# Routing ops of a mixture-of-experts kernel trimmed and interleaved, and one expert's weight loads moved behind a gather

## The chip, the cores and the metric

The kernel runs on one core of a Trainium2 chip. The metric is the device time of one execution in microseconds (us), the median over the runs. TensorE (PE) does matmuls and transposes, VectorE (DVE) and ScalarE (ACT) elementwise work, GpSimd (POOL) issues the indirect transfers, and SyncE (SP) issues most of the others. Engines meet only at semaphores.

## The reference, cut to what matters

One layer of a diffusion model over 640 tokens of width 1024 (512 latent, 128 context). After attention, convolution and a LayerNorm, every token passes through a hierarchical mixture of experts: the best of 4 groups, then the two best of the group's 4 experts.

```
g_prob = softmax(t @ wg + bg);  g_p, g_idx = top_k(g_prob, 1)
e_prob = softmax(take_along_axis(e_logits, g_idx)); e_p, e_idx = top_k(e_prob, 2)
ids = g_idx * 4 + e_idx
hid = einsum("nd,edf->nef", t, w_exp_in); a, up = split(hid, 2)
out = einsum("nef,efd->nd", silu(a) * up * gate, w_exp_out)
```

The kernel does not compute all 16 experts for all tokens. It makes for each expert a list of up to 128 tokens, gathers their rows, and works on these alone.

## The kernel before

Everything is written out by hand: the order of the instructions on each engine is that of the code, and waits are on counted semaphores. Matrices are split into a high and a low part (`w_hi` on ACT, `w_lo` on DVE), and three products stand for one.

The 640 tokens are five tiles of 128, n = 0 to 4 (NT = 5). In the stage before the experts, PE computes the output projection `mix_out(n)`, DVE makes the LayerNorm of tile n out of it and then `h2`, the rows that the experts read. PE turns these (`turn_h2`), ACT copies them (`h2_copy`), PE multiplies by the router's weights (`router`, `router_fold`), and DVE chooses:

- `choose(n)` on DVE (L1477): a chain of 13 small ops in which each waits for the one before (`link`), from the logits to the one-hot of both choices, `both` and `before`, which release `rank(n)` on PE (L2210).
- `put(n)` on DVE (L1505): the token's place in its experts' lists out of `rank(n)`'s sums, `slot_hot` (for the list, `fill(n)` on PE, L2217) and `hot_0` (L1516, L1517), a one-hot of the tokens that go to expert 0. `put(2)` stands between the halves of tile 4's LayerNorm.
- `gather_first(n)` on PE (L2195): expert 0's rows are not fetched; they are summed out of the tiles in SBUF by matmuls with `hot_0`.
- The list for the experts 1 to 15 (`list_s`, L1634 and L1635) is ready after `fill(4)`.

In the experts' stage POOL fetches the rows of expert c by an indirect DMA (`gather`, L743) from the DRAM copy of h2, which POOL stored tile by tile (L735). The gather of expert 1 waits for the stores of all tiles, for the list, and for ACT's last `normed`. When it has landed (`s_hg[1]`), PE turns the rows (`turn_rows(1)`, L2277), ACT and DVE split them (`gathered_hi`, `gathered_lo`, L1074 and L1608), and so on, with `down(c - 1)` at the end of each round. Before that, PE has the sums of expert 0 (`up_first(0, 0, 0)` and `up_first(0, 0, 1)`, L2290 to L2302), whose low parts DVE makes in four pieces, the last behind a wait for the issue of gather 1 (`s_gi`, L1649).

SP issues in one queue, in the order of the code: `expert_in(e, h)` half h (1 MB) of expert e's input weights, into one of 7 half homes (L567); `expert_out(e)` (1 MB, L593); `x1_away(j)` (1 MB, L607), which puts away rows whose space the halves of experts 4 and 5 take. `expert_in(5, 0)` waits until both have landed.

Of the kernel before, what the change touches and what calls it, by code (L numbers as in the profile page):

```python
# [5 lines left out]
def build(nc, ins, outs):  # L6
# [6 lines left out]
    ALU = mybir.AluOpType  # L13
# [8 lines left out]
    P = 128  # L22
# [28 lines left out]
    NR = 24  # L51
# [21 lines left out]
    with ctx:  # L73
# [114 lines left out]
        e_num = cols[:, 10:10 + 2 * NT].rearrange("p (t c) -> p t c", t=NT)  # L188
        e_at = cols[:, 20:28].bitcast(mybir.dt.uint32)
        g_num = cols[:, 28:29]  # L190
        over_hot = raw[:, 1, 0:2 * NT * P].rearrange("p (i s) -> p i s", i=2 * NT)
# [276 lines left out]
        def _(sp):  # L468
# [757 lines left out]
        def _(dve):  # L1226
# [249 lines left out]

            def choose(n):  # L1477

                lg = logits[:, n, :]
# [3 lines left out]
                link(V.tensor_tensor(lg, PS[:, 2 if n == NT - 1 else 6, 0:NR], rb[:, :], ALU.add))  # L1483
                link(V.max(g_top[:, n, :], lg[:, 0:E_AT]))
                link(V.max_index(g_at, g_top[:, n, :], lg[:, 0:E_AT]))
# [3 lines left out]
                link(V.max(e_top[:, n, :], e_open))  # L1489
                link(V.max_index(e_at, e_top[:, n, :], e_open))  # L1490
                link(V.tensor_copy(e_num[:, n, :], e_at[:, 0:2]))
                link(V.tensor_tensor(OH[:, n], const[:, C_NUM:C_NUM + NE].unsqueeze(1).to_broadcast([P, 2, NE]),
                                     e_num[:, n, :].unsqueeze(2).to_broadcast([P, 2, NE]), ALU.is_equal))
                if n == 0:
                    link(V.memset(before[:, 0, :], 0.0))
                else:
                    dve.wait_ge(s_pos, n)
                link(V.tensor_tensor(both[:, n % 2, :], OH[:, n, 0, :], OH[:, n, 1, :], ALU.add))
# [6 lines left out]
            def put(n):  # L1505

                dve.wait_ge(s_pos, n + 1)
                src = PS[:, 3 if n == NT - 1 else 6, 32:32 + NE]
                link(V.tensor_tensor(at_pos, OH[:, n], src.unsqueeze(1).to_broadcast([P, 2, NE]), ALU.mult))
                link(V.tensor_reduce(place[:, n, :], at_pos, AX.X, ALU.add))  # L1510
# [4 lines left out]
                dve.wait_ge(s_plr, n + 1)  # L1515
                link(V.tensor_scalar(hot_0[:, n, :], slot_hot[:, n % 2, 0, :], OH[:, n, 0, 0:1], None, ALU.mult))  # L1516
                V.scalar_tensor_tensor(out=hot_0[:, n, :], in0=slot_hot[:, n % 2, 1, :], scalar=OH[:, n, 1, 0:1],  # L1517
                                       in1=hot_0[:, n, :], op0=ALU.mult, op1=ALU.add).then_inc(s_o0, 1)

# [106 lines left out]

            choose(NT - 2)
            choose(NT - 1)
            put(NT - 2)
            put(NT - 1)  # L1630

# [229 lines left out]
        def _(pe):  # L1861
# [598 lines left out]
```

## Time and profile before

| | |
|---|---|
| median of 3 runs | 547.34 us (546.74 to 547.47) |
| the profiled execution | 547.61 us, of which its span is 545.7 us |
| PE busy | 508.2 us (93%) |
| DVE busy | 435.9 us (80%) |
| ACT busy | 272.7 us (50%) |
| POOL busy | 100.0 us (18%) |
| DRAM and SBUF traffic | 142.35 MB, mean 261 GB/s |

Busy shares are means over stages with different limits. Times within the run are microseconds from the span's start. The experts' stage lies between about 350 and 505, the routing between 299 and 349.

### The profile page before, as it was taken

The page shows a single profiled execution, that of the slowest core. Times are in us where ns is not written, and L with a number is a line of the kernel's source. Part 1 is how long each engine was busy: PE and PEld are TensorE (multiplying, and loading weights), DVE is VectorE, ACT ScalarE, POOL GpSimd, SP SyncE. Part 2 cuts the span into 40 slices and gives each one's busy share as a digit, 9 for nine tenths or more (in the row PEclk, how much of TensorE's full clock was granted, in tenths as well). Part 3 has the DMA queues.
Part 4 walks back from the last instruction along what each step waited for, and adds up shares of the span by engine and source line. Part 5 has one row for each costly group of instructions (what it writes and reads, how often), then busy time and mean ns, then how long its engine had stood idle before and what let it go on. Part 6 is the DMA issues. An engine that isn't in the chain of part 4 may idle for free.

```text
span 545.7 us, 8067 instructions
## 1 busy us (share of the span) xinstructions
PE 508.2 (93%) x3137; PEld 420.8 (77%) x3138; DVE 435.9 (80%) x691; ACT 272.7 (50%) x366; POOL 100.0 (18%) x114
## 2 busy tenths in 40 slices
PE   4999999999999999999999999999999999999660
PEld 1579999997799998777887788877888888887220
DVE  3127799989698913899459879989999999997895
ACT  2236501103031303998612224767888889884273
POOL 0004900003000000231000000211534333312311
PEclk9999999999999999999999999999999999999796
DMA  8997996628958550323689109989999999997578
GB/s 296 387 387 246 235 343 188 230 78 257 372 166 297 178 155 22 79 60 85 188 317 341 74 40 347 422 317 393 389 389 369 379 401 356 378 336 312 206 253 168
DMA packets 56829, 142.35 MB, mean 261 GB/s; under 512 B 8375, under 2 KB 17138, under 8 KB 50904
## 3 DMA queue, kind: packets, MB, share of 16 engines
q1 hardware_dynamic: 44792, 119.06, 60.5%
q0 software_dynamic: 9120, 20.80, 12.8%
q10 hardware_dynamic: 2880, 1.98, 1.2%
q8 instruction: 25, 0.41, 0.3%
q14 instruction: 12, 0.10, 0.1%
HBM read 129.71 MB, written 20.20 MB: 275 GB/s over the span
## 4 chain that ended last, share of the span: by engine, by line
PE 64%; DVE 21%; DMA 8%; issue 3%; ACT 2%; POOL 0%; SPq 0%; POOLq 0%; DVEq 0%; ACTq 0%
PE PS L1866 8%; PE PS L1964 8%; PE PS L1868 8%; PE PS L1867 8%; PE PS L1969 8%; PE PS L1965 8%; DVE uni L1288 4%; PE PS L2277 2%; PE PS L2083 2%; PE PS L1893 2%; DMA raw<-in_w_ada 2%; DMA h_rows<-uni 2%; PE PS L2100 2%; PE PS L1886 2%; DVE w_lo L1530 1%
## 5 line engine op out<-in xcount | busy, mean ns | idle before, releaser
L1866 PE MATMUL PS<-w_hi,act_hi 128*128 128x512 f32 x244 | 98.7, 405 | 0.9 <-DVE act_lo L1624 0.9
L1964 PE MATMUL PS<-act_hi,w_hi 128*128 128x320 f32 x320 | 97.5, 313 | 0.2 <-issue 0.2
L1965 PE MATMUL PS<-act_lo,w_hi 128*128 128x320 f32 x320 | 96.3, 309 | 0.0
L1868 PE MATMUL PS<-w_hi,act_lo 128*128 128x512 f32 x244 | 95.4, 391 | 0.0
L1867 PE MATMUL PS<-w_lo,act_hi 128*128 128x512 f32 x244 | 95.2, 390 | 0.0
L1288 DVE SCALAR_TENSOR_TENSOR uni<-raw,uni 128x512 f32<-128x512 f32 x112 | 75.1, 745 | 0.0
L1969 PE MATMUL PS<-act_hi,w_lo 128*128 128x320 f32 x320 | 72.9, 309 | 0.0
L1964 PEld LDWEIGHTS PS<-act_hi,w_hi 128*128 128x128 f32 x320 | 60.1, 188 | 4.3 <-issue 3.6
L1965 PEld LDWEIGHTS PS<-act_lo,w_hi 128*128 128x128 f32 x320 | 60.1, 188 | 0.0
L811 ACT ACTIVATE w_hi<-raw 128x2048 fp32r<-128x2048 f32 x14 | 26.4, 1915 | 58.1 <-PE PS L1969 50.2
L1866 PEld LDWEIGHTS PS<-w_hi,act_hi 128*128 128x128 f32 x244 | 45.9, 188 | 11.8 <-issue 1.9
L1868 PEld LDWEIGHTS PS<-w_hi,act_lo 128*128 128x128 f32 x244 | 45.8, 188 | 10.1
L1969 PEld LDWEIGHTS PS<-act_hi,w_lo 128*128 128x128 f32 x320 | 53.5, 188 | 0.0
L1867 PEld LDWEIGHTS PS<-w_lo,act_hi 128*128 128x128 f32 x244 | 45.9, 188 | 8.4
L750 POOL DMA_INDIRECT expert_rows<-uni,cols x15 | 27.1, 1809 | 83.7 <-ACT uni L1092 83.7
L1530 DVE TENSOR_TENSOR w_lo<-raw,w_hi 128x2048 fp32r<-128x2048 f32 x16 | 36.5, 2286 | 0.4
L1254 DVE TENSOR_TENSOR w_lo<-raw,w_hi 128x2048 fp32r<-128x2048 f32 x14 | 31.6, 2285 | 5.5 <-ACT w_hi L811 5.5
L721 POOL DMA_DIRECT2D uni<-bias_windows x24 | 15.4, 651 | 106.9 <-DVE small L1398 106.4
L1603 DVE TENSOR_TENSOR act_lo<-uni,act_hi 128x2048 fp32r<-128x2048 f32 x14 | 32.1, 2290 | 1.7 <-ACT act_hi L1068 1.6
L1398 DVE CUSTOM_DVE_ANT_1 PS<-PS,uni 128x512 f32<-128x512 f32 x32 | 21.4, 715 | 14.7 <-issue 7.6
L1055 ACT ACTIVATE w_hi<-raw 128x2048 fp32r<-128x2048 f32 x16 | 30.5, 1909 | 0.0
L743 POOL DMA_INDIRECT uni<-h_rows,cols x15 | 23.3, 1552 | 30.5 <-PE PS L2277 18.8
(285 smaller groups left out, 934.3 us busy)
## 6 DMA issues: line engine op xcount, KB each, us to landing
raw<-in_w_ada SPq DMA_DIRECT2D x20, 1024.0 KB, 7.5
raw<-in_w_expert_in SPq DMA_DIRECT2D x16, 1024.0 KB, 12.1
uni<-in_w_expert_out SPq DMA_DIRECT2D x15, 1024.0 KB, 11.1
raw<-in_w_in SPq DMA_DIRECT2D x12, 1024.0 KB, 7.6
g<-in_w_expert_in SPq DMA_DIRECT2D x8, 1024.0 KB, 12.1
uni<-expert_rows SPq DMA_DIRECT2D x10, 512.0 KB, 7.4
uni<-in_w_ada SPq DMA_DIRECT2D x4, 1024.0 KB, 14.4
raw<-in_w_out SPq DMA_DIRECT2D x4, 1024.0 KB, 6.5
```

The source lines that it names most:

```text
L750: pool.indirect_dma_start(y_dram, bass.IndirectOffsetOnAxis(ap=list_d[:, c:c + 1], axis=0), y_sb[:, c % 2, :], None, bounds_check=2 * PAGE ...
L1055: nc.scalar.activation(w_hi[:, b, half], loaded, ACT.Copy).then_inc((s_whi, s_whp)[h], 1)
L1254: V.tensor_tensor(w_lo[:, i % 2, half], raw[:, SLOT["w", i], half], w_hi[:, i % 2, half].bitcast(fp32), ALU.subtract).then_inc(s_wlo, 1)
L1288: V.scalar_tensor_tensor(out=acc, in0=w, scalar=cond[:, k, j:j + 1], in1=acc, op0=ALU.mult, op1=ALU.add).then_inc(s_adl, 1)
L1530: V.tensor_tensor(w_lo[:, b, half], loaded, w_hi[:, b, half].bitcast(fp32), ALU.subtract).then_inc((s_wlo, s_wlp)[h], 1)
L1603: V.tensor_tensor(ol, loaded.rearrange("p (k n) -> p k n", k=2), oh.bitcast(fp32), ALU.subtract).then_inc(s_olo, 1)
L1866: T.matmul(out, lh, rh, start=first, stop=False)
L1867: T.matmul(out, lh, rl, start=False, stop=False)
L1868: return T.matmul(out, ll, rh, start=False, stop=last)
L1964: T.matmul(out, a, h_hi[:, k, sl], start=f, stop=False)
L1965: T.matmul(out, a, h_lo[:, k, sl], start=False, stop=False)
L1969: mm = T.matmul(out, b, h_hi[:, k, sl], start=False, stop=l)
```

## The change

It has three parts. On SP, `expert_out(1)` now stands first behind the wait for gather 1's landing, and both halves of expert 4's input weights stand behind it too. On DVE, `choose` loses two casts (the indices are compared as integers; one cast for all tiles moves to `token_slots`), `hot_0` comes out of one op on a one-column rank (`first_rank`, `first_hot`) instead of two on `slot_hot`, and waits are put behind independent ops; the last tile's `choose` and tile 3's `put` are interleaved (`choose_last`). On PE, two filler matmuls (`warm(1)`) go, the first half of `gather_first(3)` moves ahead of `rank(4)`, and the second half ahead of `fill(4)`.

```diff
@@ SP
+            sp.wait_ge(s_hg[1], 16)
+            expert_out(1)
             expert_in(4, 0)
+            x1_away(1)
             expert_in(4, 1)
-            sp.wait_ge(s_hg[1], 16)
-            x1_away(1)
-            expert_out(1)
             expert_in(5, 0)
...
@@ choose(n), before
-                link(V.tensor_copy(g_num, g_at[:, 0:1]))
-                link(V.tensor_scalar(e_open, const[:, C_GROUP:C_GROUP + NE], g_num, -3.0e38, ALU.not_equal, ALU.mult))
-                link(V.tensor_tensor(e_open, e_open, lg[:, E_AT:NR], ALU.add))
...
-                link(V.tensor_copy(e_num[:, n, :], e_at[:, 0:2]))
@@ after
+                return step(V.tensor_tensor(e_open, const[:, C_GROUP:C_GROUP + NE], g_at[:, 0:1].to_broadcast([P, NE]),
+                                            ALU.not_equal))
...
+                return step(V.scalar_tensor_tensor(out=e_open, in0=e_open, scalar=-3.0e38, in1=logits[:, n, E_AT:NR],
+                                                   op0=ALU.mult, op1=ALU.add))
...
+            def first_rank(n):
+
+                dve.wait_ge(s_pos, n + 1)
+                return step(V.scalar_tensor_tensor(out=first_place[:, n:n + 1], in0=rank_of(n)[:, 0:1], scalar=1.0,
+                                                   in1=both[:, n % 2, 0:1], op0=ALU.add, op1=ALU.mult))
+
+            def first_hot(n):
+
+                V.tensor_scalar(hot_0[:, n, :], const[:, C_COL:C_COL + P], 1.0, first_place[:, n:n + 1], ALU.add,
+                                ALU.is_equal).then_inc(s_o0, 1)
...
+            def put(n):
+
+                a = first_rank(n)
+                b = ranks(n)
+                after(a)
+                first_hot(n)
+                after(b)
+                after(places(n))
+                slot_hots(n)
+
+            def choose_last():
+
+                n, m = NT - 1, NT - 2
+                a = logits_of(n)
+                b = first_rank(m)
+                after(a)
+                a = group_top(n)
+                after(b)
+                first_hot(m)
+                after(a)
+                a = group_at(n)
+                b = ranks(m)
...
@@ token_slots
+                link(V.tensor_copy(e_num, e_at[:, :, 0:2]))
@@ PE, after router_fold(4) and rank(3)
             gather_first(2)
-            warm(1)
+            gather_first(NT - 2, (0,))
             rank(NT - 1)
-            warm(1)
+            T.matmul(PS[:, 6, 64:64 + NE], ones[:, :], before[:, NT % 2, :], start=True, stop=True).then_inc(s_cnt, 1)
             fill(NT - 2)
-            pe.wait_ge(s_one, NT)
-            T.matmul(PS[:, 6, 64:64 + NE], ones[:, :], before[:, NT % 2, :], start=True, stop=True).then_inc(s_cnt, 1)
-            gather_first(NT - 2, (0,))
+            gather_first(NT - 2, (1,))
             fill(NT - 1)
-            gather_first(NT - 2, (1,))
             gather_first(NT - 1, (0,))
```

On SP, at the start of the experts' stage (`raw`, `g` and `uni` with `w_expert_in` are expert 3's second half, expert 4's first and second half and expert 5's first), the order changes so:

```order
 L593 DMA uni<-in_w_expert_out 128x2048 [waits h2_tile_0_stored,h2_transposed,h2_ready]
 L567 DMA raw<-in_w_expert_in 128x2048 [waits h2_ready]
+L593 DMA uni<-in_w_expert_out 128x2048 [waits h2_tile_2_stored,h2_tile_1_stored,h2_transposed,rows_transposed_for_expert,h2_ready,rows_gathered_1]
 L567 DMA g<-in_w_expert_in 128x2048 [waits x1_rows_put_away_or_back]
+L607 DMA x_rows<-g 128x2x1024 [waits normed_ready]
 L567 DMA uni<-in_w_expert_in 128x2048 [waits normed_ready,logits_by_group_ready]
-L607 DMA x_rows<-g 128x2x1024 [waits normed_ready,rows_gathered_1]
-L593 DMA uni<-in_w_expert_out 128x2048 [waits h2_tile_1_stored,h2_tile_2_stored,rows_transposed_for_expert,h2_transposed,h2_ready]
 L567 DMA g<-in_w_expert_in 128x2048 [waits x1_rows_put_away_or_back]
```

The wait `rows_gathered_1` (gather 1 has landed) now stands ahead of four transfers of 1 MB where it stood ahead of two.

On DVE, this is the end of the last tile's `choose` and the `put` of tile 3 before (L1509 reads the ranks, L1513 writes `slot_hot`, L1516 and L1517 write `hot_0`):

```order
L1490 MAX_INDEX cols<-uni 128x8 [waits vector_chain]
L1491 CAST cols<-cols 128x2 [waits vector_chain]
L1492 TENSOR_TENSOR uni<-const,cols 128x32 [waits vector_chain]
L1498 TENSOR_TENSOR uni<-uni 128x16 [waits positions_of_tile_ready,vector_chain]
L1499 TENSOR_TENSOR uni<-uni 128x16 [waits vector_chain]
L1502 TENSOR_TENSOR uni<-uni,const 128x32 [waits list_of_tile_added]
L1509 TENSOR_TENSOR uni<-uni,PS 128x32 [waits positions_of_tile_ready]
L1510 TENSOR_REDUCE cols<-uni 128x2 [waits vector_chain]
L1513 TENSOR_TENSOR uni<-const,cols 128x256 [waits list_of_tile_added,vector_chain]
L1516 TENSOR_SCALAR uni<-uni 128x128 [waits places_of_tile_ready]
L1517 SCALAR_TENSOR_TENSOR uni<-uni 128x128 [waits vector_chain]
```

The same place in the changed kernel begins with the last tile's logits (L1496); L1561 and L1566 are tile 3's `first_rank` and `first_hot`, L1571 and L1575 its `ranks` and `places`:

```order
L1496 TENSOR_TENSOR logits<-PS,rb 128x24 [waits logits_sum_ready]
L1561 SCALAR_TENSOR_TENSOR cols<-PS,uni 128x1 [waits positions_of_tile_ready]
L1500 MAX uni<-logits 128x8 [waits vector_chain]
L1566 TENSOR_SCALAR uni<-const,cols 128x128 [waits vector_chain]
L1504 MAX_INDEX uni<-uni,logits 128x8 [waits vector_chain]
L1571 TENSOR_TENSOR uni<-uni,PS 128x32
L1508 TENSOR_TENSOR uni<-const,uni 128x16 [waits vector_chain]
L1575 TENSOR_REDUCE cols<-uni 128x2 [waits vector_chain]
L1513 SCALAR_TENSOR_TENSOR uni<-uni,logits 128x16 [waits vector_chain]
L1518 MAX uni<-uni 128x8 [waits vector_chain]
L1522 MAX_INDEX uni<-uni 128x8 [waits vector_chain]
L1526 TENSOR_TENSOR uni<-const,uni 128x32 [waits vector_chain]
```

Tile 3's four ops have moved up between the last tile's, and the last tile's MAX now stands behind an op that waits for PE's `rank(3)`.

On PE, after `rank(3)`, this stood before (L2205 is `gather_first`, L2214 and L2215 `rank(4)`, L2221 `fill`, L2256 the counts, L2237 `warm`):

```order
L2205 MATMUL PS<-uni 128x128 [waits first_expert_one_hot_ready]
L2205 MATMUL PS<-uni 128x128 x7
L2237 MATMUL PS<-const 128x256
L2214 MATMUL PS<-uni,const 128x16 [waits choices_of_tile_ready]
L2215 MATMUL PS<-uni,rows 128x16
L2237 MATMUL PS<-const 128x256
L2221 MATMUL PS<-uni 128x16 [waits places_of_tile_ready]
L2221 MATMUL PS<-uni 128x16
L2256 MATMUL PS<-uni,rows 128x16 [waits choices_of_tile_ready]
L2205 MATMUL PS<-uni 128x128 [waits first_expert_one_hot_ready]
L2205 MATMUL PS<-uni 128x128 x3
L2221 MATMUL PS<-uni 128x16 [waits places_of_tile_ready]
```

And this stands there now (L2311 is `gather_first`, L2320 and L2321 `rank(4)`, L2359 the counts, L2327 `fill`):

```order
L2311 MATMUL PS<-uni 128x128 [waits first_expert_one_hot_ready]
L2311 MATMUL PS<-uni 128x128 x7
L2311 MATMUL PS<-uni 128x128 [waits first_expert_one_hot_ready]
L2311 MATMUL PS<-uni 128x128 x3
L2320 MATMUL PS<-uni,const 128x16 [waits choices_of_tile_ready]
L2321 MATMUL PS<-uni,rows 128x16
L2359 MATMUL PS<-uni,rows 128x16
L2327 MATMUL PS<-uni 128x16 [waits places_of_tile_ready]
L2327 MATMUL PS<-uni 128x16
L2311 MATMUL PS<-uni 128x128 [waits first_expert_one_hot_ready]
L2311 MATMUL PS<-uni 128x128 x3
L2327 MATMUL PS<-uni 128x16 [waits places_of_tile_ready]
```

All of tile 3's share of expert 0's sum now stands ahead of the last `fill`, and the fillers between are gone.

## Rows read from the trace of the kernel before

**Rows 1.** Waits of PE from 375 us on: line, releaser, total, times, longest.

```profile
PE PS L1866 <- DVE act_lo L1624: 1.7, 2, 0.9
```

**Rows 2.** Chain that ended last: start us, us, what.

```profile
340.08 9.36 DMA h_rows<-uni
...
350.55 7.28 DMA uni<-h_rows,cols
...
360.13 1.23 DVE act_lo L1608
...
377.20 0.50 PE PS L1866
```

**Rows 3.** Busy us by engine, TensorE's clock, DMA share, GB/s in one stretch.

```profile
350.00:355.00 5.00, 5.00 (x29) 4.37 (x29) 5.00 (x6) 4.21 (x4) 3.10 (x3) 1.00 1.00 414
```

**Rows 4.** Timeline of PE: start us, us, line, op [idle before, releaser].

```profile
302.26 0.39 PE L2214 MATMUL PS<-uni,const 128*128 128x16 f32 x2 [0.81 <-DVE uni L1499]
...
333.08 1.03 PE L2175 MATMUL PS<-const,uni 128*128 128x128 f32 x8
...
338.49 0.63 PE L2175 MATMUL PS<-const,uni 128*128 128x128 f32 x4 [0.35 <-DVE uni L1594]
...
345.46 0.40 PE L2214 MATMUL PS<-uni,const 128*128 128x16 f32 x2
...
348.40 2.92 PE L2205 MATMUL PS<-uni 128*128 128x128 f32 x24
351.17 1.03 PE L2237 MATMUL PS<-const 128*128 128x256 f32 x4
...
357.87 1.16 PE L2277 MATMUL PS<-const,uni 128*128 128x128 f32 x8 [0.21 <-DMA uni<-h_rows,cols]
```

**Rows 5.** Timeline of DVE.

```profile
325.48 0.15 DVE L1486 CAST cols<-uni 128x1 f32<-128x1 uint32 x1
325.67 0.23 DVE L1487 TENSOR_SCALAR uni<-const,cols 128x16 f32<-128x16 f32 x1
...
332.31 0.17 DVE L1509 TENSOR_TENSOR uni<-uni,PS 128x32 f32<-128x32 f32 x1
...
333.79 0.68 DVE L1569 TENSOR_TENSOR uni<-PS,raw 128x512 f32<-128x512 f32 x1
...
342.19 0.17 DVE L1499 TENSOR_TENSOR uni<-uni 128x16 f32<-128x16 f32 x1
342.29 0.18 DVE L1502 TENSOR_TENSOR uni<-uni,const 128x32 f32<-128x32 f32 x1
342.73 0.18 DVE L1483 TENSOR_TENSOR logits<-PS,rb 128x24 f32<-128x24 f32 x1 [0.26 <-PE PS L2193]
...
348.59 0.17 DVE L1634 TENSOR_SCALAR cols<-PS 128x16 f32<-128x16 f32 x1
...
353.44 1.22 DVE L1537 TENSOR_TENSOR w_lo<-w_lo_before_subtraction,w_hi 128x1024 fp32r<-128x1024 f32 x1
```

**Rows 6.** Timeline of SP's issues.

```profile
347.06 0.33 SPq L567 DMA_DIRECT2D g<-in_w_expert_in  x1
...
357.85 0.38 SPq L607 DMA_DIRECT2D x_rows<-g  x1
```

**Rows 7.** Line L750, indirect stores of expert rows, 15 of them.

```profile
DMA to landing us min/median/max: 4.0/9.1/9.9
```

**Rows 8.** Line L607, `x1_away`, from 325 to 376 us, 2 of them.

```profile
DMA to landing us min/median/max: 4.9/8.9/12.8
```

**Rows 9.** Line L593, `expert_out`, 16 of them.

```profile
DMA to landing us min/median/max: 6.5/11.2/13.7
```

**Rows 10.** Line L567, `expert_in`, 28 of them.

```profile
DMA to landing us min/median/max: 5.7/12.1/18.3
```

**Rows 11.** Timeline of ACT.

```profile
376.73 1.91 ACT L1055 ACTIVATE w_hi<-g 128x2048 fp32r<-128x2048 f32 x1
...
381.17 1.91 ACT L1068 ACTIVATE act_hi<-uni 128x2048 fp32r<-128x2048 f32 x1
```

More of the change, by code:

```diff
@@ L1475, in offset, with step, after, rank_of @@
                                        op0=ALU.mult, op1=ALU.mult).then_inc(s_v, 1)
-            def choose(n):
-                lg = logits[:, n, :]
+            def step(ins_):
+                chain[0] += 1
+                ins_.then_inc(s_dv, 1)
+                return chain[0]
+            def after(count):
+                dve.wait_ge(s_dv, count)
+            def rank_of(n):
+                return PS[:, 3 if n == NT - 1 else 6, 32:32 + NE]
+            def logits_of(n):
                 dve.wait_ge(s_lg, n + 1)
@@ L1489, in choose @@
-                link(V.max(e_top[:, n, :], e_open))
-                link(V.max_index(e_at, e_top[:, n, :], e_open))
-                link(V.tensor_copy(e_num[:, n, :], e_at[:, 0:2]))
[L1492 to L1496, printed above, removed]
+                return step(V.tensor_tensor(logits[:, n, :], PS[:, 2 if n == NT - 1 else 6, 0:NR], rb[:, :], ALU.add))
@@ new lines, in group_top, with group_at, other_groups, open_logits @@
+            def group_top(n):
+                return step(V.max(g_top[:, n, :], logits[:, n, 0:E_AT]))
+            def group_at(n):
+                return step(V.max_index(g_at, g_top[:, n, :], logits[:, n, 0:E_AT]))
+            def other_groups(n):
+                return step(V.tensor_tensor(e_open, const[:, C_GROUP:C_GROUP + NE], g_at[:, 0:1].to_broadcast([P, NE]),
+                                            ALU.not_equal))
+            def open_logits(n):
+                return step(V.scalar_tensor_tensor(out=e_open, in0=e_open, scalar=-3.0e38, in1=logits[:, n, E_AT:NR],
+                                                   op0=ALU.mult, op1=ALU.add))
@@ new lines, in expert_top, with expert_at, choices, both_choices @@
+            def expert_top(n):
+                return step(V.max(e_top[:, n, :], e_open))
+            def expert_at(n):
+                return step(V.max_index(e_at[:, n, :], e_top[:, n, :], e_open))
+            def choices(n):
+                return step(V.tensor_tensor(OH[:, n], const[:, C_NUM:C_NUM + NE].unsqueeze(1).to_broadcast([P, 2, NE]),
+                                            e_at[:, n, 0:2].unsqueeze(2).to_broadcast([P, 2, NE]), ALU.is_equal))
+            def both_choices(n):
+                if n >= 1:
@@ L1497, in choose, with counted @@
                     dve.wait_ge(s_pos, n)
-                link(V.tensor_tensor(both[:, n % 2, :], OH[:, n, 0, :], OH[:, n, 1, :], ALU.add))
+                return step(V.tensor_tensor(both[:, n % 2, :], OH[:, n, 0, :], OH[:, n, 1, :], ALU.add))
+            def counted(n):
                 V.tensor_tensor(before[:, (n + 1) % 2, :], before[:, n % 2, :], both[:, n % 2, :], ALU.add).then_inc(s_one, 1)
@@ L1503, in choose, with ranks, places, slot_hots @@
                                 const[:, C_TOK + 2 * n:C_TOK + 2 * n + 2].unsqueeze(2).to_broadcast([P, 2, NE]), ALU.mult)
-            def put(n):
-                dve.wait_ge(s_pos, n + 1)
-                src = PS[:, 3 if n == NT - 1 else 6, 32:32 + NE]
-                link(V.tensor_tensor(at_pos, OH[:, n], src.unsqueeze(1).to_broadcast([P, 2, NE]), ALU.mult))
-                link(V.tensor_reduce(place[:, n, :], at_pos, AX.X, ALU.add))
+            def choose(n):
+                after(logits_of(n))
+                after(group_top(n))
+                after(group_at(n))
+                after(other_groups(n))
+                after(open_logits(n))
+                after(expert_top(n))
+                after(expert_at(n))
+                after(choices(n))
+                if n == 0:
+                    link(V.memset(before[:, 0, :], 0.0))
+                after(both_choices(n))
+                counted(n)
+            def first_rank(n):
+                dve.wait_ge(s_pos, n + 1)
+                return step(V.scalar_tensor_tensor(out=first_place[:, n:n + 1], in0=rank_of(n)[:, 0:1], scalar=1.0,
[3 more added lines that the diff above has]
+                                ALU.is_equal).then_inc(s_o0, 1)
+            def ranks(n):
+                return step(V.tensor_tensor(at_pos, OH[:, n], rank_of(n).unsqueeze(1).to_broadcast([P, 2, NE]), ALU.mult))
+            def places(n):
+                return step(V.tensor_reduce(place[:, n, :], at_pos, AX.X, ALU.add))
+            def slot_hots(n):
                 if n >= 2:
@@ L1514, in put @@
                                 place[:, n, :].unsqueeze(2).to_broadcast([P, 2, P]), ALU.is_equal).then_inc(s_plr, 1)
[L1515 to L1518, printed above, removed]
+            def put(n):
[17 more added lines that the diff above has]
+                b = ranks(m)
+                after(a)
+                a = other_groups(n)
+                after(b)
+                b = places(m)
+                after(a)
+                after(open_logits(n))
+                after(expert_top(n))
+                after(expert_at(n))
+                after(choices(n))
+                after(both_choices(n))
+                counted(n)
+                after(b)
+                slot_hots(m)
+                a = first_rank(n)
+                b = ranks(n)
+                after(a)
+                first_hot(n)
+                after(b)
+                after(places(n))
+                slot_hots(n)
             def expert_wlo(e, b, h):
@@ L1627, in _ @@
             choose(NT - 2)
-            choose(NT - 1)
-            put(NT - 2)
-            put(NT - 1)
+            choose_last()
             dve.wait_ge(s_ls, NT)
```

7 lines of the change are left out of this document (2 added, 5 removed).

## The prediction

> **What bounds the kernel now.** I read the waits of TensorE first, then the chain of work that ended last, then the timelines of the engines at the places of the change.
>
> From 375 us to the end of the experts, PE waited for elementwise work only twice, 1.7 us in all, each time for DVE's `act_lo` [rows 1]; one of these is at 377.20, where `down(1)` starts [rows 2]. Behind it PE is the bound, so whatever brings `down(1)` forward brings the end forward by as much, unless a load comes late. What sets `down(1)`? The chain goes back without a gap through DVE from 360.13 (`gathered_lo` of expert 1), through PE's turning of expert 1's rows at 357.87, which waited 0.21 us for gather 1 [rows 4], to that gather (issued 350.55, landed 7.28 us later) and to the store of tile 4's h2 rows (issued 340.08, landed 9.36 us later) [rows 2]. From 350 to 355 the DMA engines were full, at 414 GB/s [rows 3]. So the reader is to see three links: what DVE and PE do up to the store, two transfers in a crowd, and an unbroken piece of DVE work.
>
> Close beside this chain lies a second one: PE's fillers behind `gather_first(4)` begin at 351.17 and the sum of expert 0 runs behind them to 357.87 less the 0.21 us of waiting, 357.66 [rows 4]. A faster gather alone is worth 0.21 us. Both have to move.
>
> **The change part by part.** All shifts are against the trace of before.
>
> *`choose` shorter.* The first cast takes 0.19 us from start to start (325.48 to 325.67) and the second is like it. The compare that reads a pointer scalar takes 0.23 us busy, plain ops of that size 0.17 [rows 5]. So each `choose` loses 0.19 + 0.19 + 0.06, about 0.45 us. It counts where somebody waits. At 302.26 PE waits 0.81 us for tile 0's `choose` [rows 4]: 0.45 us for everything behind. For tile 1, DVE waits for PE later, so nothing. Tile 2's lies on DVE's chain into the last tile's LayerNorm: another 0.45 us.
>
> *`put(2)` shorter.* From 332.31 to 333.79 it takes 1.48 us [rows 5]. It will be five ops, of which three do not wait for the one just ahead. Ops that wait start 0.20 us apart, ops that don't 0.10 (342.19 to 342.29) [rows 5]. I make it 0.10 + 0.10 + 0.21 + 0.22 + 0.34, about 0.97, so 0.5 us less. But the next op needs the end of tile 4's projection: PE goes on to transposes at 333.08 [rows 4], and a sum is read about 0.2 us later, at 333.28. So of 0.45 + 0.5 only 0.51 us counts (333.79 to 333.28). With the first 0.45, DVE is 0.97 us early from there on, and tile 4's store is issued at 339.1.
>
> *PE before the last routing.* At 338.49 PE waits 0.35 us for DVE [rows 4]. It gains its own 0.45 and this 0.35: 0.8 us. The last logits come at 342.73 less 0.8.
>
> *The last routing* (in the times of before, less 0.8 at the end). `first_rank(3)` waits for `rank(3)` on PE, which runs right behind the fold that released the logits, so it starts some 0.43 us behind 342.73 (an estimate: two small matmuls of 0.2 us, the time in which a sum is read); the MAX stands behind it where it would start after 0.2, so it stalls some 0.3 us. The shorter chain gives 0.45 back, and `rank(4)` could start as before (345.46), but PE is then busy with the moved half gather and gets to it at about 345.85: 0.4 later. The removed filler with its wait gives 0.5 back. The list, at 348.59 before [rows 5], is ready at about 348.45, less 0.8: 347.6. The half gather moved out of the tail is worth (351.17 less 348.40) / 3 = 0.92 us [rows 4]. So PE's fillers start 0.95 us earlier than before, less 0.8: at 349.4. The sum of expert 0 behind them took 357.66 less 351.17 = 6.5 us and ends at 355.9. Its last low part comes from DVE at 353.44 + 1.22, less 1.0, 353.7 [rows 5], just when PE comes to it, so this is as far as PE can move.
>
> *The moved cast.* The moved cast costs 0.1 to 0.2 us on DVE in expert 4's round. What hides it is DVE's lead over PE there (of PE's two waits the one at 377.20 lies earlier and the other at the end) [rows 1]; uncovered it costs 0.2.
>
> *Expert 4's weights behind gather 1.* The store of tile 4 has the same crowd in front of it as before (the 2 MB were issued only at 347.06 [rows 6] and after): 339.1 + 9.36 = 348.5. POOL took 1.1 us from that landing to the gather's issue (349.44 to 350.55) [rows 2]: issue at 349.6. How long does the gather take without the 2 MB? The trace has no lone gather. Above: 7.28 as now [rows 2]. Below: 4.0, the quickest indirect store of as many rows, in an empty stretch [rows 7]. The 2 MB are 2.1 / 414 = 5.1 us of full DMA engines, and DMA will have drained what is older by about 350, so I take 4.5 (3.3 us at most are missing to the upper end). Landing at 354.1, before PE is free at 355.9. The gather stops being last; `turn_rows(1)` starts at 355.7 to 355.9, against 357.87.
>
> *What is late next.* Behind SP's wait now stand `expert_out(1)`, both halves of expert 4 and `x1_away(1)`, 4 MB from 354.1, and behind them `expert_in(5, 0)` and `expert_out(2)`. The first half of expert 4 was issued at 347.06 and is now at 354.4. ACT reads it at 376.73 less 2.1 = 374.6 [rows 11]; with the slowest landing of its kind, 18.3 us [rows 10], it is there at 372.7. Cost nothing.
>
> **The sum.** Everything from `turn_rows(1)` on is 2.0 to 2.2 us earlier, and DVE's unbroken chain carries it to `down(1)`. I take 2.1. The profiled execution took 547.61 us, 0.27 over the median of 547.34. 547.61 less 2.1 is 545.5; against the median, **545.2 us** (0.38%).
>
> *A rule against this.* What an op without a wait saves is 0.10 us of 0.20 in the rows [rows 5]. The Trainium skill, "VectorE: DVE Perf Modes", § "The DRAIN you can't avoid", says that the flush between ops cannot be skipped by chaining them without semaphores. By it the interleaved ops would cost their full length and the time would be that of rival 2, 546.0. The two rows at 342.19 and 342.29 speak for the overlap, which is why I give it little.
>
> **Rivals.**
>
> 1. *The gather stays last.* If its 7.28 us are not the crowd's doing, it lands at 349.6 + 7.3 = 356.9 against 357.83: 0.9 us, 546.4. If the store of tile 4 also lands no earlier than 349.4, nothing but 0 to 0.2 is left, 547.2. For it: gather 1's own rows are small pieces. Against: full DMA engines up to 355 [rows 3], 4.0 us in an empty stretch [rows 7]. Chance 0.2.
>
> 2. *Interleaved ops don't overlap.* Then tile 3's four ops delay the last tile's chain by some 0.7 us, `rank(4)` starts 0.4 later still, and the list, on which DVE's low parts for expert 0 hang, comes about 0.8 later. The end moves by 2.1 less 0.8 = 1.3: 546.0. Chance 0.12.
>
> 3. *Slower: SP's queue.* `x1_away(1)` took 4.9 us in a thin stretch, its sister 12.8 in a full one [rows 8]. Now it is issued at about 355.2 in a full one. If it takes 12.8, `expert_in(5, 0)` goes at 368.0 and `expert_out(2)` at 368.4. ACT wants that at 381.17 less 2.1 = 379.1 [rows 11]. The slowest such load took 13.7 us [rows 9]: 382.1, 3.0 us late, and the kernel ends 0.9 us above before, 548.2. It decides from 12.8 us of landing for `expert_out(2)` on to be slower than before (from 10.7 on it eats the gain). Against: only 4 MB are ahead (10 us). Chance 0.08.
>
> **Chances and range.** The forecast has 0.6, with a range of its own of 544.6 to 545.8: down if DVE's op savings are larger or the PE chain moves by more than its own sum, up if the cast or the last low part holds PE for some tenths. A measurement here can tell about 0.2%, 1.1 us, from no change (547.34 less 1.1 = 546.2). Faster by more: all but a little of the forecast, most of rival 2, a quarter of rival 1: 0.58 + 0.09 + 0.05 = 0.72. Slower: most of rival 3, 0.07. The rest is within: 0.21. The range takes in rivals 2 and the first form of 1: 544.4 to 546.8 leaves out the second form of 1, rival 3 and tails of the forecast, 0.2 in all.
>
> **What would show it.** Right: PE's wait at 302 down from 0.81 to about 0.36; DVE at 342.7 some 0.8 earlier; gather 1 landing in under 5.5 us from its issue, before PE ends expert 0's sum, so that no engine waits for it; `turn_rows(1)` near 355.8; expert 4's half issued near 354.4 and nobody waiting for it. Wrong: PE idle before `turn_rows(1)` with the DMA as releaser (rival 1); starts 0.2 us apart inside the interleaved ops (rival 2); ACT idle before an `expert_out` copy or `expert_in` copy between 375 and 400 (rival 3). What would upset the sum, too, is a wait of DVE for the issue of gather 1 ahead of its last low part for expert 0 (at 353.44 less 1.0): that happens if the gather goes no earlier than before.

## The result, and the profile after

The changed kernel took **550.89 us** (median of 7 runs) against 547.68 us for the kernel before in the same job: ratio 1.0051, interval 1.0029 to 1.0073. It is slower by 0.5%, and 545.2 was forecast. One of its runs took 2834.69 us, as one each of e1 and e2 below took 1289.61 and 2537.32, and nothing here rests on those three (without its own the changed kernel's median is 550.5). The profiled execution took 552.03 us, its span 550.0 against 545.7.

Up to 375 us the profile is the one that was forecast. PE's timeline at tile 0's `rank`, at the end of the fillers and expert 0's sum, and at `down(1)` (columns as in [rows 4]):

```profile
302.07 0.40 PE L2320 MATMUL PS<-uni,const 128*128 128x16 f32 x2 [0.36 <-DVE uni L1537]
...
349.31 1.03 PE L2343 MATMUL PS<-const 128*128 128x256 f32 x4
...
355.71 1.05 PE L2380 MATMUL PS<-const,uni 128*128 128x128 f32 x8
...
374.92 0.50 PE L1972 MATMUL PS<-act_hi 128*128 128x512 f32 x1 [0.75 <-DVE act_lo L1731]
```

The wait at 302 fell from 0.81 to 0.36 us, the fillers start at 349.31 (forecast 349.4), `turn_rows(1)` at 355.71 (forecast 355.7 to 355.9) waits for nobody, and `down(1)` starts 2.28 us earlier than in [rows 2]. POOL's timeline and the landing of gather 1 (line L743, the one issue at 349):

```profile
339.41 0.53 POOL L735 DMA_DIRECT2D h_rows<-uni  x1 [8.87 <-DVE uni L1701]
349.44 1.74 POOL L743 DMA_INDIRECT uni<-h_rows,cols  x1 [9.50 <-issue]
```

```profile
DMA to landing us min/median/max: 5.0/5.0/5.0
```

From there the two kernels part. The chain that ended last (columns as in [rows 2]) leaves DVE at 374.56 for a load:

```profile
372.33 2.21 DVE act_lo L1710
374.56 18.84 DMA uni<-in_w_expert_out
393.42 1.92 ACT act_hi L1068
```

ACT, whose waits view of before had no load from 375 on, and PE behind it (timelines):

```profile
393.42 1.91 ACT L1068 ACTIVATE act_hi<-uni 128x2048 fp32r<-128x2048 f32 x1 [4.78 <-DMA uni<-in_w_expert_out]
```

```profile
398.05 0.80 PE L1972 MATMUL PS<-act_hi 128*128 128x512 f32 x1 [3.87 <-DVE act_lo L1731]
```

After those 3.87 us of waiting PE's clock was granted at half, 1.2 GHz of 2.4 (windows; the clock's share is the third column from the right, as in [rows 3]), and `down(3)` took 5.15 us instead of 2.7:

```profile
394.00:396.00 2.00, 0.18 (x1) 0.00 (x0) 0.63 (x1) 2.00 (x3) 0.00 (x0) 1.00 0.99 416
396.00:398.00 2.00, 0.00 (x0) 0.00 (x0) 2.00 (x3) 2.00 (x2) 0.00 (x0) 0.55 1.04 432
398.00:400.00 2.00, 1.95 (x5) 1.57 (x6) 2.00 (x2) 2.00 (x3) 0.00 (x0) 0.50 0.95 379
```

The lead of 2.28 less 3.87 of wait less 2.45 of slow clock makes 4.0 us behind, and the spans are 4.3 apart. Why does a load issued *earlier* than before (374.56; before 376.84, landing after 9.8 us) land after 18.8? SP's timeline (which answers to [rows 6]) shows what was put in front of it:

```profile
354.50 0.33 SPq L593 DMA_DIRECT2D uni<-in_w_expert_out  x1
354.88 0.42 SPq L567 DMA_DIRECT2D g<-in_w_expert_in  x1
355.36 0.42 SPq L607 DMA_DIRECT2D x_rows<-g  x1
355.88 0.76 SPq L567 DMA_DIRECT2D uni<-in_w_expert_in  x1
368.98 0.33 SPq L567 DMA_DIRECT2D g<-in_w_expert_in  x1
369.35 0.43 SPq L593 DMA_DIRECT2D uni<-in_w_expert_out  x1
369.82 2.87 SPq L567 DMA_DIRECT2D raw<-in_w_expert_in  x3
374.56 0.33 SPq L593 DMA_DIRECT2D uni<-in_w_expert_out  x1
```

`x1_away(1)` (355.36) took 13.6 us to land. `expert_in(5, 0)`, which waits for it, held SP until 368.98 (before: 362.79), and then 5 MB went out in under 4 us, ahead of `expert_out(3)`. Meanwhile the DMA engines had been partly idle twice (shares of 0.45 and 0.70 from 350 to 358, of 0.77 from 366 to 370). The windows of the kernel before, and then of the changed one (last column GB/s):

```profile
350.00:354.00 4.00, 4.00 (x25) 3.56 (x25) 4.00 (x5) 3.21 (x4) 3.10 (x3) 1.00 1.01 418
354.00:358.00 4.00, 3.79 (x18) 2.82 (x17) 3.42 (x8) 1.58 (x3) 0.00 (x0) 1.00 0.66 265
...
366.00:370.00 4.00, 4.00 (x19) 3.26 (x18) 3.96 (x5) 3.47 (x4) 0.62 (x1) 1.00 1.01 419
...
346.00:374.00 28.00, 27.54 (x156) 23.44 (x156) 25.74 (x34) 18.89 (x21) 7.22 (x6) 1.00 0.93 366
374.00:502.00 128.00, 126.64 (x615) 105.74 (x613) 121.80 (x106) 106.88 (x94) 41.55 (x24) 1.00 0.96 374
```

```profile
350.00:354.00 4.00, 4.00 (x19) 3.24 (x18) 4.00 (x6) 3.40 (x4) 2.66 (x3) 1.00 0.45 117
354.00:358.00 4.00, 3.75 (x22) 2.96 (x21) 3.33 (x10) 1.58 (x3) 0.47 (x1) 1.00 0.70 224
...
366.00:370.00 4.00, 4.00 (x19) 3.25 (x18) 3.96 (x5) 3.47 (x3) 0.54 (x1) 1.00 0.77 312
...
346.00:374.00 28.00, 27.75 (x151) 23.41 (x150) 26.25 (x30) 20.45 (x22) 8.34 (x7) 1.00 0.83 304
374.00:502.00 128.00, 123.38 (x590) 103.09 (x590) 116.88 (x103) 103.52 (x90) 37.45 (x23) 0.97 0.97 377
```

By 374 us the changed kernel has moved (366 less 304) x 28 us = 1.74 MB less, and from there on both move about the same, 374 and 377 GB/s at a DMA share of 0.96 and 0.97. 1.74 MB at 375 GB/s are 4.6 us.

**The theory** after this reading: in the experts' stage the DMA engines have as little to spare as PE. Time that they stand idle at its start comes back as late `expert_out` loads, and PE time that is saved there is of no use. **The rivals:** SP's head-of-line wait alone (SP waits for one transfer's condition, and everything behind it in its queue waits too); the granted clock; the routing edits being worth less than they look.

### The profile page after: what moved, and what is told of

Same layout as the page of the kernel before. It is cut to its first block, busy times and chain, and to the rows that moved or that the text cites. A ratio compares the mean times of both kernels' runs of the same rounds, so it can differ in the third digit from the quotient of the medians.

```text
span 550.0 us, 8050 instructions
## 1 busy us (share of the span) xinstructions
PE 509.2 (93%) x3133; PEld 421.6 (77%) x3134; DVE 432.0 (79%) x682; ACT 272.2 (49%) x366; POOL 96.5 (18%) x114
## 4 chain that ended last, share of the span: by engine, by line
PE 73%; DVE 13%; DMA 6%; ACT 3%; issue 2%; POOL 0%; SPq 0%; POOLq 0%; DVEq 0%; ACTq 0%
PE PS L1972 10%; PE PS L1973 9%; PE PS L1974 9%; PE PS L2070 9%; PE PS L2075 9%; PE PS L2071 9%; DMA uni<-in_w_expert_out 3%; PE PS L2189 2%; PE PS L1999 2%; PE PS L2380 2%; PE PS L2311 2%; PE PS L2206 2%; PE PS L1992 2%; DVE w_lo L1637 1%; DVE act_lo L1710 1%
## 5 line engine op out<-in xcount | busy, mean ns | idle before, releaser
L750 POOL DMA_INDIRECT expert_rows<-uni,cols x15 | 25.8, 1720 | 91.8 <-ACT uni L1092 91.8
L1068 ACT ACTIVATE act_hi<-uni 128x2048 fp32r<-128x2048 f32 x14 | 26.7, 1908 | 4.8 <-DMA uni<-in_w_expert_out 4.8
```

The lines of the kernel that those rows point to most:

```text
L1068: nc.scalar.activation(home, out_home(e).rearrange("p (k n) -> p k n", k=2), ACT.Copy).then_inc(s_ohi, 1)
```

## The experiments

All were run on the chip with the kernel before beside them. "Last copy" is the start of ACT's copy of the last expert's result (501.75 before, 505.94 in the changed kernel), the end of the experts' stage.

Single profiles of the same code differ already ahead of the place of SP's change. The store of tile 4's rows is issued between 337.96 and 339.41 in the ten kernels with the routing edits, and between 339.10 and 340.81 in the four without. So a difference of under 1.7 us between the absolute times of two profiles proves nothing by itself.

**1 and 2. One part alone.** e1 is the changed kernel with SP's order of before; e2 is the kernel before with SP's new order. The diff is e1's, against the changed kernel; e2 makes the opposite edit to the kernel before.

```diff
             expert_in(3, 1)
+            expert_in(4, 0)
+            expert_in(4, 1)
             sp.wait_ge(s_hg[1], 16)
-            expert_out(1)
-            expert_in(4, 0)
             x1_away(1)
-            expert_in(4, 1)
+            expert_out(1)
             expert_in(5, 0)
```

> The changed kernel with SP's order of before; the routing edits stay. Theory (debt of the DMA engines): the loss comes from SP's order alone, so the stall at 398 is gone, expert_out(3) lands in about 10 us instead of 18.8, and the routing edits give what they moved: gather 1 issued near 349.5 and landing 7.3 us later, turn_rows(1) near 356.8, the end about 0.9 to 1.1 us before the kernel before: 546.5. Rival (the routing edits themselves cost, by the fillers taken from PE or the shorter lead): no faster than before, 547.5 or more, and the stall at 398 stays.

Measured: 547.75 us, ratio 0.9997 (0.9982 to 1.0012), as before; 546.5 was expected, with 7.3 us for the gather. PE's timeline of it:

```profile
357.38 1.16 PE L2380 MATMUL PS<-const,uni 128*128 128x128 f32 x8 [1.86 <-DMA uni<-h_rows,cols]
```

The gather was issued at 349.09 and landed 8.2 us later, with two 1 MB loads issued at 346.07 and 347.16 in front of it. In a crowd it lands when the crowd is through, as rival 1 had it, and the routing edits by themselves are worth 0.5 us at `down(1)` (less than two profiles can differ by) and nothing that can be measured in the time.

> The kernel before with the changed order on SP alone. Theory (debt): DMA engines near empty from 350 on while SP waits for gather 1, the loads of the rounds behind land in 18 to 19 us, ACT waits for expert_out(3), PE for some 3 us and then runs at the lower clock for a while; the kernel ends 3 to 6 us later than before: 550.5 to 553.5, worse than the whole change by what the routing gives. Rival (the stall comes only because the routing edits brought PE forward): no stall or one under 2 us, 547 to 549.

Measured: 552.84 us, ratio 1.0075 (1.005 to 1.0101). The whole loss is SP's order; the intervals do not tell whether it is more than the changed kernel's 1.0051. ACT's waits from 375 to 505:

```profile
ACT act_hi L1068 <- DMA uni<-in_w_expert_out: 8.7, 6, 2.7
```

**3. Is it the clock?** e3 puts eleven fillers in front of `down(3)`, so that PE works through the stall.

```diff
                 up_half(c, c % 2, 1)
+                if c == 4:
+                    warm(11)
                 down(c - 1, (c - 1) % 2)
```

> The whole change, and 11 filler matmuls of 256 columns on PE ahead of the down product of expert 3, where PE idles 3.87 us. If part of the loss is the clock that falls after the idle stretch (the down product takes 5.1 us instead of 2.7 there), the granted clock stays at its upper level and the kernel is some 2.4 us faster than the whole change, near 548.0. If the clock is not at fault, the fillers change nothing: within 0.3 us of the whole change, 550.5.

Measured: 550.89 us, ratio 1.0055 (1.0031 to 1.008). That it is the changed kernel's median to the hundredth is chance; the ratios, 1.0055 and 1.0051, agree. The clock stayed at 1.00 over the whole stage:

```profile
374.00:502.00 128.00, 126.31 (x612) 105.49 (x613) 115.47 (x102) 102.57 (x88) 44.50 (x23) 1.00 0.97 373
```

What it gave went into further waits for loads (ACT, timeline):

```profile
393.52 1.91 ACT L1068 ACTIVATE act_hi<-uni 128x2048 fp32r<-128x2048 f32 x1 [5.47 <-DMA uni<-in_w_expert_out]
...
403.43 1.91 ACT L1068 ACTIVATE act_hi<-uni 128x2048 fp32r<-128x2048 f32 x1 [1.19 <-DMA uni<-in_w_expert_out]
...
460.92 1.91 ACT L1068 ACTIVATE act_hi<-uni 128x2048 fp32r<-128x2048 f32 x1 [1.96 <-DMA uni<-in_w_expert_out]
```

Seven waits, 10.5 us, where the changed kernel had one of 4.8. So the slow clock is a form that the loss takes, not a second loss.

**4. Only one half behind the gather.**

```diff
+            expert_in(4, 0)
             sp.wait_ge(s_hg[1], 16)
             expert_out(1)
-            expert_in(4, 0)
             x1_away(1)
             expert_in(4, 1)
```

> The whole change, but expert 4's first half is asked for ahead of the wait, as before. Theory (debt): 1 MB instead of 2 MB is held back, about 2.5 us less of idle DMA, so loads behind land in 13 to 16 us, ACT's slack of 14 us for expert_out(3) nearly or wholly covers it, PE's wait falls from 3.9 us to under 1.5; gather 1 lands in 5 to 6 us, still ahead of PE. Total 545.5 to 547. Rival (SP's head of line: expert_in(5, 0) waits for the put-away that shares the queue with it, and holds expert_out(2) and more): the put-away still goes behind gather 1 and expert_out(1), lands near 366, and the stall stays above 2.5 us, total 549 or more.

Measured: 551.7 us, ratio 1.0059 (1.0036 to 1.0082): `down(1)` came at 373.47, 3.7 us earlier than before (2.1 of that stand already in the store of tile 4, 337.96 against 340.08), and ACT still waited 4.07 us for `expert_out` at 391.25. `x1_away(1)` and `expert_in(5, 0)` went at 354.08 and 366.18, 12.1 us apart where the changed kernel had 13.6, so SP was held nearly as long. In total, half of what was moved has all of the harm. The expectation named for the theory (545.5 to 547) missed, and the rival's held.

Not all of that loss lies in the experts' stage. Its last copy is 1.75 us later than before, its span 4.6 us longer. The rest comes behind it, with a second load that had no room: the rows that `x1_away` put away come back (`g<-x_rows`, L613) at 503.2 in the kernel before (issued 492.31, landed after 10.9 us), and DVE starts on them at 503.24. In e4 they were issued at 494.59 and landed after 11.6 us (DVE, timeline):

```profile
506.25 5.76 DVE L1945 TENSOR_TENSOR g<-g,uni 128x1024 f32<-128x1024 f32 x5 [1.24 <-DMA g<-x_rows]
```

That is 3.0 us later than before. What makes up the remaining 1.6 us was not separated.

**5 to 8. Taking SP's hold away, and filling the idle time.** e5 puts `x1_away(1)` ahead of the wait for gather 1; e6 puts it first behind it (these two and e8 wait for the first put-away ahead of the second, and not at `expert_in(4, 0)`); e7 lets expert 4's halves go when POOL has issued gather 1 (`s_gi`); e8 lets everything go then.

```diff
 e5                          e6                          e7                          e8
 sp.wait_ge(s_x1b, 16)       sp.wait_ge(s_hg[1], 16)     sp.wait_ge(s_gi, 1)         sp.wait_ge(s_gi, 1)
 x1_away(1)                  sp.wait_ge(s_x1b, 16)       expert_in(4, 0)             sp.wait_ge(s_x1b, 16)
 sp.wait_ge(s_hg[1], 16)     x1_away(1)                  expert_in(4, 1)             x1_away(1)
 expert_out(1)               expert_out(1)               sp.wait_ge(s_hg[1], 16)     expert_out(1)
 expert_in(4, 0)             expert_in(4, 0)             x1_away(1)                  expert_in(4, 0)
 expert_in(4, 1)             expert_in(4, 1)             expert_out(1)               expert_in(4, 1)
 expert_in(5, 0)             expert_in(5, 0)             expert_in(5, 0)             expert_in(5, 0)
```

> The whole change, but x1_away(1) stands ahead of the wait for gather 1 (it goes as soon as x1_away(0) has landed and its rows are ready, near 347); expert_out(1) and expert 4's two halves stay behind it. The debt theory says that two gaps of the DMA engines cost time: the one while SP waits (350 to 356) and a second one near 369, where SP is held at expert_in(5, 0) by the landing of the put-away. Here 1 MB fills half of the first gap and the second is gone: expert_in(5, 0) goes near 355, expert_out(3) lands in under 14 us and ACT hardly waits for it; total 545.5 to 547.0. If only the bytes held back matter (still 2 MB of expert 4), the loads still land late: 549 or more.

> The whole change, but x1_away(1) is the first behind the wait for gather 1, ahead of expert_out(1) and expert 4's halves. The first gap (SP waiting) stays as it is, the second (SP held at expert_in(5, 0)) should shrink, for the put-away lands near 361 instead of 369. By the two-gap theory total 548.0 to 549.5, between the whole change and before; if the second gap is worth nothing, as the whole change, 550.5; if it is all, 546.

> The whole change, but expert 4's two halves wait for gather 1's issue (near 351) instead of its landing; x1_away(1) and expert_out(1) wait for the landing, in the order of before. The debt theory: the DMA engines idle only from 350 to 352, no late loads behind. If the gather keeps the place that it got by being issued first, it lands in 5 to 6.5 us, before PE ends expert 0's sum, and both gains stay: 545.3 to 546.3. If a gather lands only when the transfers that crowd it have drained, whatever their order, it lands near 357 and PE waits: 547 to 548, no better than before.

> The whole change, but all of SP's queue (x1_away(1), expert_out(1), expert 4's halves) waits for the issue of gather 1 only, the put-away first. The most DMA work as early as possible behind the gather: no debt, expert_in(5, 0) near 360. If the gather keeps its place: 545.0 to 546.3. If the crowd behind delays it (4 MB, 10 us): it lands near 359 to 361, turn_rows(1) 2 to 3 us later than before, 549 to 551.

Measured: e5 549.41 (1.0034, 1.0018 to 1.0051), e6 550.5 (1.0053, 1.0035 to 1.0071), e7 549.65 (1.0038, 1.0024 to 1.0051), e8 548.2 (1.0012, 0.9996 to 1.0029). None came out as the debt theory had it. e5 and e6 came out at their other branch ("549 or more"; "550.5"), e7 and e8 at neither of theirs.

Gather 1 kept its place when other transfers were issued *behind* it: in e7 (two loads of 1 MB from 350.75 on) and in e8 (4 MB from 350.77 on) it landed in 5.2 us. The gather of expert 2, issued at 350.90 with these around it, took 10.4 us in both, and PE waited for it (e8, PE's timeline):

```profile
361.35 0.82 PE L2381 MATMUL PS<-const,uni 128*128 128x128 f32 x5 [0.79 <-DMA uni<-h_rows,cols]
```

The hold is gone in e5 (`expert_in(5, 0)` at 355.93) and is 2.7 us or less in e6 and e8 (`expert_in(5, 0)` at 360.87 and 357.06). e6, which still starts everything behind gather 1, lost as much as the changed kernel all the same. In e5 `down(1)` is 2.7 us early, and still nothing is gained: the lead at the result copy of each round shrinks from 2.7 us (396.51 in e5, 399.23 before) to nothing at the last (501.90 against 501.75), in waits for `expert_out` of 5.0 us. So SP's hold is not the whole of it. In e5 the tail lost more: DVE waited 1.5 us for the rows that come back from DRAM and started on them at 504.97. e8's windows, for the sake of their GB/s:

```profile
346.00:374.00 28.00, 26.96 (x146) 22.78 (x145) 26.29 (x29) 19.43 (x21) 10.57 (x7) 1.00 0.94 366
374.00:502.00 128.00, 125.44 (x607) 104.11 (x605) 118.90 (x105) 104.88 (x93) 43.73 (x24) 1.00 0.97 371
```

The same two numbers of each kernel, with its last copy and its span (e9 and e10 are described below):

| | GB/s 346 to 374 | GB/s 374 to 502 | last copy | span |
|---|---|---|---|---|
| before | 366 | 374 | 501.75 | 545.7 |
| e1 | 367 | 373 | 501.37 | 545.5 |
| e8 | 366 | 371 | 501.43 | 545.9 |
| e5 | 366 | 368 | 501.90 | 548.0 |
| e7 | 339 | 373 | 502.99 | 548.6 |
| e9 | 366 | 366 | 503.02 | 547.5 |
| e4 | 325 | 373 | 503.50 | 550.3 |
| e10 | 372 | 370 | 503.51 | 548.1 |
| e6 | 328 | 373 | 504.49 | 550.0 |
| e3 | 297 | 373 | 505.73 | 551.3 |
| changed | 304 | 377 | 505.94 | 550.0 |
| e2 | 293 | 377 | 506.35 | 551.6 |

Where `down(1)` stands (373.47 in e4, 376.70 in e1) says nothing of the end of the stage. In the ten kernels other than e9 and e10 the last copy goes with the bytes moved by 374: those bytes, at 375 GB/s, account for the delay of the last copy to within 1.4 us. e9 and e10 moved as many bytes by 374 as the kernel before, or more, and still ended the stage 1.3 and 1.8 us later. That the third column hardly varies is in part bookkeeping, as the same loads are moved in stages of nearly the same length. It is the DMA share (0.95 to 0.98) and the next two runs that carry the theory.

**9 and 10. Fewer bytes (e11, e12).** The test of the theory, in both kernels. From expert 4 on each half of the input weights brings only half of its rows, and the kernel leaves the rest out; it computes those experts with old numbers, in the same instructions. 12.6 MB are gone, all of them experts' weights: some 22% of the 58 MB moved from 346 to 502, not the 40% of the expectation below.

```diff
-                sp.dma_start(home.rearrange("p (k n) -> p k n", k=4), src[:, 4 * h:4 * h + 4, :]).then_inc(landed, 16)
+                k = 2 if e >= 4 else 4
+                sp.dma_start(home.rearrange("p (k n) -> p k n", k=4)[:, 0:k, :], src[:, 4 * h:4 * h + k, :]).then_inc(landed, 16)
```

> The changed kernel, but from expert 4 on each half of the input weights brings only two of its four row blocks (0.5 MB of 1 MB; the other half of each home keeps old numbers, so the experts' sums are not the reference's). It is to be read against the same cut of the kernel before. Theory: the loss comes from the DMA engines having no spare time in the experts' stage, so that time left idle at 350 to 358 and 366 to 372 comes back as late expert_out loads. With some 40% of the stage's bytes gone the loads land in time, ACT waits nowhere for expert_out, and the 2.28 us that down(1) is earlier last to the end: 2.0 to 2.7 us less than the light kernel before (about 545.0 against 547.3). Rival: the loss is in the queue's order alone (SP held at expert_in(5, 0) by the landing of x1_away(1)) or in compute (the clock, DVE's order); then the light changed kernel keeps most of its 3 us loss against the light kernel before, 549 or more.

> The kernel before with the same cut (from expert 4 on each half of the input weights brings 0.5 MB of 1 MB; the sums of those experts are not the reference's). The kernel before has no wait for a weight load from 375 on, so fewer bytes have nothing to give there: both theories say as the kernel before, 547.0 to 547.8; perhaps some tenths less by gather 1, no more than 0.5. If it is 2 us faster or more, the loads held the kernel before too, in a way that its waits do not show.

Measured: **545.3 us** for the light changed kernel (0.997, 0.9945 to 0.9996) and 547.47 for the light kernel before (1.0011, 0.9997 to 1.0024). The medians are 2.17 us apart, where 2.1 was the prediction's sum; with these intervals that is 2.2 us give or take some 1.6 (an estimate from their widths), so that it agrees so closely is partly luck. SP's and PE's timelines of the light changed kernel:

```profile
353.77 0.42 SPq L608 DMA_DIRECT2D x_rows<-g  x1
354.29 0.47 SPq L568 DMA_DIRECT2D uni<-in_w_expert_in  x1
364.07 0.33 SPq L568 DMA_DIRECT2D g<-in_w_expert_in  x1
```

```profile
373.51 0.50 PE L1973 MATMUL PS<-act_hi 128*128 128x512 f32 x1 [0.77 <-DVE act_lo L1732]
```

In the light kernel before `down(1)` is at 375.75, 2.24 later; the last copies are at 498.17 and 500.28, 2.11 apart. The lead lasts, and neither kernel waits for a load from 375 to 505; the DMA share is 0.80 and 0.82 (windows of the light changed kernel, then of the light kernel before):

```profile
374.00:502.00 128.00, 126.87 (x616) 105.77 (x614) 121.12 (x108) 104.70 (x93) 43.02 (x25) 1.00 0.80 289
374.00:502.00 128.00, 126.27 (x614) 105.50 (x613) 121.10 (x107) 106.19 (x93) 40.55 (x24) 1.00 0.82 290
```

SP is still held for 9.8 us here, by the same wait, and no wait for a load follows from it. The light kernel before has its `down(1)` 1.45 us earlier than the full one and its profiled execution is 1.1 us shorter, while the medians are the same (547.47, 547.45). Of that 0.98 us stand already in the store of tile 4 (339.10 against 340.08), ahead of the first load that brings less (345.76), so most of it is a difference between two executions.

**11 and 12. The same bytes in another order (e9, e10).** For the experts 6 to 9 `expert_out(e - 3)` goes ahead of the second input half, in e8's kernel (e9) and in the kernel before (e10).

```diff
                 expert_in(e, 0)
-                if 10 <= e <= 13:
+                if e <= 13:
                     expert_out(e - 3)
                 expert_in(e, 1)
-                if e < 10:
-                    expert_out(e - 3)
...
```

> The variant with all of SP's transfers at gather 1's issue, and in the experts 6 to 9 expert_out(e - 3) is issued ahead of the second input half of expert e instead of behind it. The full byte count is kept. If the 2.7 us lead of that variant is lost only because each expert_out stands behind 1 MB more of weights that nobody needs yet, each lands some 2.5 us earlier, ACT's waits at 398, 408 and 419 (0.8, 1.8, 1.7 us) go, and the end is 545.0 to 546.5 (0.2 to 0.5% under the kernel before). If the DMA engines' bytes are the limit, whatever their order, the waits only move to a later load (an input half, a gather or an expert_out of the experts 10 to 15) and it stays at 547.5 to 548.5.

> The kernel before with that order of the issues alone (expert_out(e - 3) ahead of the second input half for the experts 6 to 9). Nothing waits for expert_out in the kernel before, so both theories say no change, 547.3 to 547.9; the landings of expert_out(3) to expert_out(6) should be some 2.5 us quicker than their 9.8 to 13.7.

Measured: 548.43 us (1.0023, 1.0003 to 1.0042) and 549.51 (1.0036, 1.0017 to 1.0056). In e9 the waits at 398 to 419 are gone and stand later (ACT, timeline):

```profile
426.84 1.91 ACT L1067 ACTIVATE act_hi<-uni 128x2048 fp32r<-128x2048 f32 x1 [1.30 <-DMA uni<-in_w_expert_out]
...
437.30 1.92 ACT L1067 ACTIVATE act_hi<-uni 128x2048 fp32r<-128x2048 f32 x1 [1.76 <-DMA uni<-in_w_expert_out]
...
447.98 1.91 ACT L1067 ACTIVATE act_hi<-uni 128x2048 fp32r<-128x2048 f32 x1 [1.95 <-DMA uni<-in_w_expert_out]
```

That is what the theory said of e9. For e10 it said no change, and that was wrong. `expert_out(3)` (377.40) landed in 7.3 us instead of 9.8, as expected, but it waits for its slot, and `expert_in(6, 1)` now stands behind it. ACT waited for `expert_out` twice (2.0 us), the last copy came 1.8 us later than before (0.7 of it stands already in the store of tile 4, 340.81), and from 374 to 502 e10 moved 370 GB/s and e9 366. That those holds are what cost the time fits, but no run separates it. No variant with the full bytes beat the kernel before; e1 and e8 can't be told from it.

## Why the prediction was wrong, by its own steps

- **What bounds the kernel: half right.** "Behind it PE is the bound, so whatever brings `down(1)` forward brings the end forward by as much, unless a load comes late." `down(1)` came 2.28 us forward and the end went back. The waits of [rows 1] name only PE and DVE, and from that I took it that loads had room. The room could be read: a DMA share of 0.96 from 374 to 502, and the slowest `expert_out` landing at 13.7 us [rows 9]. That one was issued at 441.79 and read by ACT at 456.20, 14.4 us later, so 0.7 us were to spare.
- **`choose`, `put(2)`, PE before the last routing: right.** Wait at 302 0.36, store at 339.41 (forecast 339.1), gather issue 349.44 (349.6).
- **The last routing and PE's chain: right**, the stall at `first_rank(3)` 0.26 us (0.3), list at 347.63 (347.6).
- **Interleaved ops (rival 2): refuted.** They start 0.08 to 0.12 us apart in DVE's timeline, so the rule of the Trainium skill, "VectorE: DVE Perf Modes", § "The DRAIN you can't avoid", did not cost here what I worked out from it. The prediction told only half of that section, which also says that a next op that is not held starts earlier; the trace agrees with that half:

```profile
342.96 0.16 DVE L1504 FIND_INDEX8 uni<-uni,logits 128x8 uint32<-128x8 f32 x1
343.04 0.17 DVE L1571 TENSOR_TENSOR uni<-uni,PS 128x32 f32<-128x32 f32 x1
343.16 0.18 DVE L1508 TENSOR_TENSOR uni<-const,uni 128x16 f32<-128x16 f32 x1
```

- **Gather 1 without the 2 MB: right**, 5.0 us for 4.5. (From 4.5 to the upper end of 7.28 it is 2.8 us; the prediction's 3.3 counts from the lower end. Nothing hangs on it.) e1 shows that rival 1's mechanism is real where the crowd stays.
- **"What is late next": the step that failed.** I asked only whether expert 4's half itself would be in time (it was: landed 10.7 us after 354.88, used at 374) and wrote "Cost nothing". The price was not in that transfer but in the engines' time: 2 MB held back until gather 1 had landed left them at 117 GB/s from 350 to 354, and everything queued behind is that much later. The bytes missing by 374, 1.74 MB or 4.6 us, are about what the stage lost (4.2 us at the last copy). What was late was not the half that moved but `expert_out(3)`: 18.8 us of landing, ACT 4.78 us late, PE 3.87.
- **Rival 3: right place, wrong price and chance.** `expert_in(5, 0)` went at 368.98 (rival: 368.0) and `expert_out(2)` at 369.35 (368.4), but that one landed in 9.4 us. The late one was `expert_out(3)`, behind 5 MB that the hold had bunched. "Against: only 4 MB are ahead (10 us)" was too little for the put-away in this order: it took 13.6 us, and 6.4 and 6.3 where it went first (e5, e8). And the light kernels show that the hold costs nothing when fewer bytes are to be moved, while e5, e6 and e8 show no gain without it or with little of it. It is a way in which DMA time is lost, not the limit itself.
- **The sum: right as PE's sum**, as far as the intervals tell: 2.17 us of gain with 22% of the stage's bytes taken away. It was the sum of one resource of two.

## What to carry to other kernels

Where a stage streams weights at a DMA share near 1, count its bytes as a second chain beside the compute: divide them by the measured GB/s, and compare with the length of the stage before you give a gain on the first chain to the end. In such a stage, holding a transfer back so that a small one lands sooner was paid for here by whichever load had the least slack between its issue and its use, rounds later; look for that load (the largest landing against its issue-to-use time), not at the one you moved. No wait in the profile of before is no sign of room.

## What the runs showed of the hardware that was not expected

- A gather of 128 rows (0.5 MB) landed in 8.2 us with two 1 MB loads issued 2 to 3 us before it (e1) and in 5.0 us without; from a second queue it was not served ahead of them. With 2 to 4 MB issued from 1.5 to 1.8 us *behind* it on, it landed in 5.2 us (e7, e8).
- With the full bytes the experts' stage moved 366 to 377 GB/s from 374 to 502 us in all twelve kernels, at a DMA share of 0.95 to 0.98; a window of 2 us reached 432 (396 to 398 in the changed kernel).
- PE idle for 3.87 us was granted 0.50 of its clock for its next 5 us of work; when that was prevented, the kernel's time did not change.
